# Loading, first norm, first modulation columns and input projection in one stage

## The chip, the cores and the metric

The kernel runs on one core of a Trainium2 chip. The core has TensorE (PE in the rows, with PEld for its weight loads), VectorE (DVE), ScalarE (ACT), GpSimd (POOL) and SyncE (SP, used here for issuing DMAs). The metric is the device time of one run in microseconds (us). The kernel before takes 2195.86 us, the median of three runs (2195.0 to 2195.89).

## The reference, cut to what matters

Two transformer blocks of two layers each are computed for 256 latent tokens and 256 context tokens of width 1024. The change touches only the first steps of the first layer. In the reference they are:

```
m_l = (silu(c) @ mod_w + mod_b)[:, None, :]        # 6 x 1024 values; shift and scale come first
m_c = silu(c_ctx) @ mod_w + mod_b
sh1_l, sc1_l, g1_l, sh2_l, sc2_l, g2_l = jnp.split(m_l, 6, axis=-1)
p_lat = _ada(x, norm1, sh1_l, sc1_l) @ w_in        # _ada = rmsnorm(x, g) * (1 + scale) + shift
p_ctx = _ada(ctx, norm1, sh1_c, sc1_c) @ w_in      # w_in is 1024 x 3328
```

## The kernel before

Activations lie transposed: a tile holds 128 of the 1024 features in its partitions and all 512 tokens in its free dimension, so XT, HT and OT have 8 tiles each (KT = 8) and PT has 32. Weights stream from memory through RING, which has four slots (SLOTS = 4); a slot holds 1024 x 256 weights, 1 MB. Matmuls of the projections are done in three passes for precision: a weight slot and the operand are each split into a rounded high part and a rest (high and low), and the passes are high by high, high by low and low by high (three_passes, L627 ff.). Of a slot there are two halves m, each with 8 k-tiles by 3 passes, 24 matmuls of 512 columns. The first input projection has 13 slots, so 26 halves and 624 matmuls.

The program is a row of stages. A stage (class Stage) is a block in which each engine has its own instruction list; at its end all engines meet, and no instruction of the next stage starts before. The first three stages are:

- load_stage (L358 ff.). SP issues the constants (1.4 MB), the tokens x and ctx (four tiles of 0.5 MB), the first four slots of the modulation weights (mod.fetch, L667), and WDG. ACT issues 31 small DMAs of vectors (rows of ROWS), c and c_ctx among them, then applies Silu to c and c_ctx. POOL issues 24 small DMAs. TensorE waits for the constants and for all 31 rows, transposes the three row tiles (L440), then waits for the tokens and transposes them (L447, 32 transposes). VectorE copies the results out of the PSUM banks (L457, L460), and derives small vectors, LAM among them.
- first_ada_stage (L713 ff.). ACT squares XT (L737), TensorE sums the squares with a matrix of ones (L752), ACT makes the root with Ln and Exp (L2611, L2617), DVE multiplies (L763). TensorE then adds up the modulation columns, one slot after another (Modulation.add, L678, 16 records a slot), each followed by a copy of the sums on ACT (copy, L686) and by small matmuls that turn them into columns (fold, L691). SP refills a ring slot when its sums are done: slots 4 to 7 of the modulation, then the first four slots of the projection's weights. At the end DVE forms MOD and AFF (L701, L708), and DVE (5 tiles, L771) and ACT (3 tiles, L746) scale and shift HT.
- project_stage (L781 ff.). ACT makes the high part of the first half slot (L560), then the high parts of the eight operand tiles (L564, OT_rounded); DVE makes the rests (L590 for the weights, L582 for the operand, HT_rounded). TensorE starts with the first tile of these (L632 to L634). The halves of weight slots alternate between two high buffers; ACT takes each finished bank to PT (L798). Some of the loop turns run in a hardware loop (turns).

After them comes diff_prepare_stage (L2411 ff.), and everything behind it is not touched. A class Part, used for the projections of later stages, does what project_stage does in straight-line code, with four high buffers (high4) and matmuls on L880 to L882.

Order is set by semaphores and by the order of the instructions on each engine; nothing reorders them at run time.

Of the kernel before, what the change touches and what calls it, by code (L numbers as in the profile page):

```python
# [34 lines left out]
P = 128  # L35
# [21 lines left out]
C_OVER = C_EPS + 4  # L57
# [10 lines left out]
C_FOLD = C_SINA + LAT  # L68
N_CONST = C_FOLD + 2

# [287 lines left out]
def load_stage(net, mod):  # L358

    nc, ins = net.nc, net.ins  # L360
    rows = net.SC[:, 0:3 * P].rearrange("p (g m) -> p g m", m=P)
    tokens = net.PT[:, 0:2 * NCH, :].rearrange("p t m -> p (t m)").rearrange("p (t d) -> p t d", d=D)
    with Stage(net, "load") as st:
        const_in, rows_in, x_in = st.sem("const_in"), st.sem("rows_in"), st.sem("x_in")
        small_in, zeroed = st.sem("small_in"), st.sem("wf_zeroed")
        turned, copied, cols_ready = st.sem("turned"), st.sem("copied"), st.sem("cols_ready")
        own = st.sem("dve_own")
        lam_exp, lam_sums, act_own = st.sem("lam_exp"), st.sem("lam_sums"), st.sem("act_own")
        smalls_in = net.smalls_in
        n_rows = sum(len(t) for t in ROWS)  # L370

        @st.sync
        def _(sp):
            sp.dma_start(net.CONST[:, :], ins["const_1"]).then_inc(const_in, 16)
            for t in range(2):
                sp.dma_start(tokens[:, t, :], ins["x"][0, P * t:P * t + P, :]).then_inc(x_in, 16)
            for t in range(2):
                sp.dma_start(tokens[:, 2 + t, :], ins["ctx"][0, P * t:P * t + P, :]).then_inc(x_in, 16)
            for n in range(SLOTS):
                mod.fetch(sp, n)  # L380
            w1 = ins["l1_w_in"]
            for at, col in ((0, 1536), (16, 3088)):
                sp.dma_start(net.WDG[:, :, at:at + 16],
                             w1[:, col:col + 16].rearrange("(t k) m -> k t m", k=P)).then_inc(small_in, 16)
            sp.wait_ge(small_in, 32)

        @st.scalar
        def _(act):
            n = 0
            for g, tile in enumerate(ROWS):  # L390
                r = 0
                for name, count in tile:
                    a = ins[name]
                    if len(a.shape) == 2:
                        a = a.rearrange("a b -> (a b)")
                    flat = a.rearrange("(t p) -> t p", p=P)
                    act.dma_start(rows[r:r + count, g, :], flat).then_inc(rows_in, 16)
                    r += count
            link = Chain(act, act_own)

            act.wait_ge(cols_ready, 3)
            act.wait_ge(zeroed, 2)
            for n, name in enumerate(("c", "c_ctx")):
                act.activation(mod.c[:, :, n], net.PAR[:, COL[name]:COL[name] + 8], ACT.Silu)

            act.wait_ge(lam_sums, 1)
            act.activation(net.LAM[:, 2:4], net.LAM[:, 0:2], ACT.Exp).then_inc(lam_exp, 1)

        @st.gpsimd
        def _(pool):  # L410
            pool.memset(net.WF[:, :, :, :], 0.0).then_inc(zeroed, 1)
# [4 lines left out]
            for n, name in enumerate(("l1_dt_bias_f", "l1_dt_bias_b", "l1_a_log_f", "l1_a_log_b",  # L416
                                      "l1_d_skip")):
                small.append((net.HEADROW[:, 8 * n:8 * n + 8], ins[name].partition_broadcast(P)))
# [87 lines left out]
def turns(engine, w, turn, straight=False, peel=False):  # L506
# [3 lines left out]
    for i in range(first):  # L510
        turn(i, range(SLOTS))
# [3423 lines left out]
```

## Time and profile before

| | before |
|---|---|
| median of 3 runs | 2195.86 us |
| profiled execution: own time / span | 2197.19 / 2195.40 us |
| busy share: TensorE, weight loads, VectorE, ScalarE, GpSimd | 89%, 77%, 55%, 38%, 14% |
| mean granted TensorE clock over the span | 0.938 of full |
| bytes read from memory | 251.28 MB, 115 GB/s over the span |

The span runs from the first to the last instruction, and all times in rows are counted from its start. The profile page cuts the span into 40 slices of 55 us. In the first, TensorE is busy 4 tenths and the DMA engines 7; in the second and third TensorE is busy 8 and 9 tenths, as the projection runs. The shares of the page are means over all stages, and so the rows below are taken from the first 72 us and from single stretches.

### The profile page before, as it was taken

The numbers are of one execution on the slowest core, as the hardware profiler recorded it, in microseconds if no ns is written. First come the engines' busy times: TensorE is split into PE (matmuls) and PEld (weight loads), VectorE is DVE, ScalarE is ACT, GpSimd is POOL, SyncE is SP. The second block draws the span as 40 slices with busy tenths as digits, with TensorE's granted clock in tenths as the row PEclk, the third lists the DMA queues.
The fourth block names the chain that finished last, engine by engine and source line by source line (L and its number), as shares of the span: only waits on it lengthen the run. The fifth ranks groups of instructions, "written<-read, shape, count | busy, mean of one in ns | idle before, by whom it ended". The sixth has DMA issues, their size and how long they took to land. (4 is left out here: it accounts for less than half of the span.)

```text
span 2195.4 us, 42104 instructions
## 1 busy us (share of the span) xinstructions
PE 1956.1 (89%) x18071; PEld 1693.2 (77%) x18071; DVE 1218.2 (55%) x2095; ACT 828.1 (38%) x1459; POOL 304.7 (14%) x350
## 2 busy tenths in 40 slices
PE   4899787888788999999999658999899999898997
PEld 2688454776766988888978548999868999768997
DVE  2321756546346752353565657874586765577753
ACT  2322356314223331222344124553365444364432
POOL 2000302421412100001200211101103001112001
PEclk9899796997999999999999858999999999999998
DMA  7421592003014322322233005555405556314543
GB/s 221 137 95 38 192 307 97 4 4 97 4 59 136 97 96 96 96 95 89 86 115 111 5 1 165 183 188 182 150 16 163 188 163 203 116 52 153 182 158 110
DMA packets 248857, 255.00 MB, mean 116 GB/s; under 512 B 6898, under 2 KB 247170, under 8 KB 248546
## 3 DMA queue, kind: packets, MB, share of 16 engines
q1 hardware_dynamic: 247200, 251.19, 35.7%
q8 instruction: 141, 2.31, 0.4%
q0 software_dynamic: 864, 0.98, 0.2%
q14 instruction: 42, 0.34, 0.1%
q10 hardware_dynamic: 610, 0.18, 0.0%
HBM read 251.28 MB, written 1.05 MB: 115 GB/s over the span
## 5 line engine op out<-in xcount | busy, mean ns | idle before, releaser
L860 DVE TENSOR_TENSOR RING_rounded<-RING,SC_rounded 128x1024 fp32r<-128x1024 f32 (+2 forms) x364 | 429.8, 1224 | 197.3 <-ACT SC_rounded L853 196.8
L880 PE MATMUL bank<-OT_rounded,SC_rounded 128*128 128x256 f32 (+1 forms) x1600 | 494.1, 309 | 21.8 <-DVE PT L1599 11.4
L881 PE MATMUL bank<-HT_rounded,SC_rounded 128*128 128x256 f32 (+1 forms) x1600 | 490.7, 307 | 0.0
L882 PE MATMUL bank<-OT_rounded,RING_rounded 128*128 128x256 f32 (+1 forms) x1600 | 489.0, 306 | 0.0
L853 ACT ACTIVATE SC_rounded<-RING 128x1024 fp32r<-128x1024 f32 (+2 forms) x364 | 346.5, 1003 | 325.6 <-DMA RING<-in_l_mlp_w 186.4
L880 PEld LDWEIGHTS bank<-OT_rounded,SC_rounded 128*128 128x128 f32 x1600 | 306.1, 191 | 41.6 <-issue 13.5
L882 PEld LDWEIGHTS bank<-OT_rounded,RING_rounded 128*128 128x128 f32 x1600 | 306.1, 191 | 15.4
L881 PEld LDWEIGHTS bank<-HT_rounded,SC_rounded 128*128 128x128 f32 x1600 | 306.2, 191 | 13.7
L880 PE MATMUL bank<-PT_rounded,SC_rounded 128*128 128x256 f32 (+1 forms) x896 | 277.8, 310 | 4.9 <-DVE RING_rounded L860 4.9
L881 PE MATMUL bank<-PT_rounded,SC_rounded 128*128 128x256 f32 (+1 forms) x896 | 276.8, 309 | 0.0
L882 PE MATMUL bank<-PT_rounded,RING_rounded 128*128 128x256 f32 (+1 forms) x896 | 276.1, 308 | 0.0
L880 PEld LDWEIGHTS bank<-PT_rounded,SC_rounded 128*128 128x128 f32 x896 | 168.6, 188 | 16.8 <-DVE RING_rounded L860 6.1
L882 PEld LDWEIGHTS bank<-PT_rounded,RING_rounded 128*128 128x128 f32 x896 | 168.5, 188 | 10.6
L881 PEld LDWEIGHTS bank<-PT_rounded,SC_rounded 128*128 128x128 f32 x896 | 168.5, 188 | 9.4
L881 PE MATMUL bank<-OT_rounded,SC_rounded 128*128 128x256 f32 (+1 forms) x336 | 101.8, 303 | 0.0
L880 PE MATMUL bank<-HT_rounded,SC_rounded 128*128 128x256 f32 (+1 forms) x272 | 84.6, 311 | 17.4 <-DVE OT_rounded L1787 8.7
L3172 DVE TENSOR_TENSOR SC<-SC,bank 128x512 f32<-128x512 f32 (+1 forms) x80 | 51.4, 684 | 75.4 <-PE bank L3063 75.0
L632 PE MATMUL bank<-OT_rounded,SC_rounded 128*128 128x512 f32 x208 | 83.9, 403 | 7.3 <-DVE HT_rounded L582 7.3
L590 DVE TENSOR_TENSOR RING_rounded<-RING,SC_rounded 128x1024 fp32r<-128x1024 f32 x26 | 31.8, 1226 | 101.5 <-ACT SC_rounded L560 101.5
L1126 DVE SCALAR_TENSOR_TENSOR XT<-bank,MOD,XT 128x256 f32<-128x256 f32 x48 | 21.4, 481 | 115.4 <-PE bank L882 115.4
L882 PE MATMUL bank<-HT_rounded,RING_rounded 128*128 128x256 f32 (+1 forms) x272 | 83.6, 307 | 0.0
L633 PE MATMUL bank<-HT_rounded,SC_rounded 128*128 128x512 f32 x208 | 83.5, 402 | 0.0
(527 smaller groups left out, 3224.9 us busy)
## 6 DMA issues: line engine op xcount, KB each, us to landing
RING<-in_l_mlp_w SPq DMA_DIRECT2D x64, 1024.0 KB, 5.2
RING<-in_l_mod_w SPq DMA_DIRECT2D x48, 1024.0 KB, 6.5
RING<-in_w_ffn_in SPq DMA_DIRECT2D x44, 1024.0 KB, 5.1
RING<-in_l_w_in SPq DMA_DIRECT2D x25, 1024.0 KB, 5.4
RING<-in_w_ffn_out SPq DMA_DIRECT2D x16, 768.0 KB, 4.4
RING<-in_w_in SPq DMA_DIRECT2D x10, 1024.0 KB, 5.3
RING<-in_w_ffn_out SPq DMA_DIRECT2D x16, 640.0 KB, 4.2
RING<-in_l_w_out SPq DMA_DIRECT2D x8, 1024.0 KB, 5.3
```

What stands on the lines that cost most here:

```text
L590: net.nc.vector.tensor_tensor(low, whole, net.high(s, m)[:, 0:w.kts[s], :].bitcast(F32), ALU.subtract).then_inc(sems.split_ready[m], 1)
L632: net.nc.tensor.matmul(bank[:, 0:n], high, x_high, start=start, stop=False)
L633: net.nc.tensor.matmul(bank[:, 0:n], high, x_low, start=False, stop=False)
L853: act.activation(net.high4(s, m)[:, 0:self.w.kts[s], :], net.ring_half(net.RING, s, m, self.w.kts[s]), ACT.Copy).then_inc(self.high_ready, 1)
L860: net.nc.vector.tensor_tensor(low, whole, net.high4(s, m)[:, 0:self.w.kts[s], :].bitcast(F32), ALU.subtract).then_inc(self.split_ready, 1)
L880: net.nc.tensor.matmul(bank[:, tokens], high, x_high, start=start, stop=False)
L881: net.nc.tensor.matmul(bank[:, tokens], high, x_low, start=False, stop=False)
L882: return net.nc.tensor.matmul(bank[:, tokens], low, x_high, start=False, stop=stop)
L1126: return nc.vector.scalar_tensor_tensor(into, bank[:, tokens], net.MOD[:, gate + tile, j:j + 1], into, ALU.mult, ALU.add)
L3172: nc.vector.tensor_tensor(inv, inv, bank, ALU.subtract).then_inc(doubled, 1)
```

## The change

The three stages become one, first_stage. In it:

- The constants are loaded in two pieces: the first 646 columns (330 KB, identity, ones, epsilons and the fold columns, which moved ahead for this) come first, the rest after the first four weight slots of the projection. WDG is loaded there too.
- c and c_ctx are waited for alone and turned first. 13 of the 31 row DMAs are issued by ACT before it waits for them, 18 after the Silu.
- The tokens are transposed into six banks (0 to 5). TensorE adds modulation slot 0 right behind them, then the squares of tiles 0 to 3, slot 1, the squares of tiles 4 to 7, slots 2 and 3, then transposes the three row tiles, then slots 4 to 7.
- ACT shifts the odd tiles of HT, DVE the even ones, tile by tile, each followed by its high part (ACT) and rest (DVE). The projection's first weight slot is split after tile 0, its second after tile 5.
- The first slot of the projection runs k-tile by k-tile with both halves side by side, each k-tile as its operand tile is ready. The other 12 slots run as halves. Part is used in place of project_stage, with four high buffers and six banks, in straight-line code.
- LAM's Exp moves behind the first slot of the projection.

The diff, cut (load_stage, first_ada_stage, project_stage and their helpers go; first_stage is new):

```diff
@@ constants @@
-C_OVER = C_EPS + 4
+C_FOLD = C_EPS + 4
+C_OVER = C_FOLD + 2
@@ first_stage @@
+        part = Part(net, st, "in0", w_in, Operand(OR, HR), banks=6)
+        @st.sync
+        def _(sp):
+            sp.dma_start(net.CONST[:, 0:C_OVER], ins["const_1"][:, 0:C_OVER]).then_inc(const_in, 16)
+            for n, name in enumerate(("x", "ctx")):
+                for t in range(2):
+                    sp.dma_start(tokens[:, 2 * n + t, :], ins[name][0, P * t:P * t + P, :]).then_inc(x_in, 16)
+            for n in range(n_first):
+                if n >= SLOTS:
+                    sp.wait_ge(mod.summed, n - SLOTS + 1)
+                mod.fetch(sp, n)
+            for s in range(SLOTS):
+                sp.wait_ge(mod.summed, n_first - SLOTS + s + 1)
+                net.fetch(sp, w_in, 0, s)
+            sp.dma_start(net.CONST[:, C_OVER:N_CONST], ins["const_1"][:, C_OVER:N_CONST]).then_inc(late_in, 16)
...
+            part.fetch_all(sp, None)
+            sp.wait_ge(late_in, 48)
...
+        @st.tensor
+        def _(pe):
+            pe.wait_ge(const_in, 16)
+            pe.wait_ge(c_in, 32)
+            nc.tensor.transpose(net.ps[6][:, 0:16], rows[0:16, 0, :], ident[0:16, 0:16]).then_inc(c_turned, 1)
+            pe.wait_ge(x_in, 64)
+            for f in range(KT):
+                if f >= 6:
+                    pe.wait_ge(copied, f - 5)
+                for t in range(4):
+                    last = nc.tensor.transpose(net.ps[f % 6][:, P * t:P * t + P],
+                                               tokens[:, t, P * f:P * f + P], ident)
+                last.then_inc(turned, 1)
+            pe.wait_ge(c_ready, 2)
+            mod.add(pe, 0, 0)
+            squares(range(4))
+            mod.add(pe, 1, 0)
+            squares(range(4, KT)).then_inc(summed, 1)
+            mod.add(pe, 2, 0)
+            mod.add(pe, 3, 0)
+            pe.wait_ge(rows_in, 16 * n_rows)
+            pe.wait_ge(copied, 6)
+            for g, tile in enumerate(ROWS):
...
+            for n in range(4, n_first):
+                mod.add(pe, n, 0)
+            mod.fold(pe, n_first - 1, 0)
+            for m in range(2):
+                part.ready(pe, 0, m)
+            for kt in range(KT):
+                pe.wait_ge(split_ready, kt + 1)
+                for m in range(2):
+                    step = part.passes(0, m, kt, everything)
...
+            for q in range(1, part.total):
+                for m in range(2):
+                    part.half(pe, q, m, everything)
+        @st.scalar
+        def _(act):
+            fetch_rows(places[:13])
+            act.wait_ge(c_turned, 1)
+            act.wait_ge(zeroed, 1)
+            for n in range(2):
+                act.activation(mod.c[:, :, n], net.ps[6][:, 8 * n:8 * n + 8], ACT.Silu).then_inc(c_ready, 1)
+            net.log_exp_loaded = False
+            fetch_rows(places[13:])
+            for t in range(KT):
+                act.wait_ge(copied, t + 1)
+                act.activation(square[:, t, :], net.XT[:, t, :], ACT.Square).then_inc(squared, 1)
+                if t == 3:
+                    mod.copy(act, 0)
+            load_log_exp(net, act)
+            mod.copy(act, 1)
+            mod.copy(act, 2)
+            act.wait_ge(summed, 1)
+            link(act.activation(rstd, total, ACT.Ln, scale=1.0 / D, bias=net.eps(EPS)))
+            act.activation(rstd, rstd, ACT.Exp, scale=-0.5).then_inc(rstd_ready, 1)
+            for n in range(3, n_first):
+                mod.copy(act, n)
+            act.wait_ge(aff_ready, 1)
+            for t in range(KT):
+                if t in by_act:
...
+                act.activation(OR[:, t, :], HT[:, t, :], ACT.Copy).then_inc(high_ready, 1)
+                if t in (0, 5):
+                    highs(t // 5)
+            for q in range(part.total):
+                highs(q + 2)
...
+        @st.vector
+        def _(dve):
...
+            link(mod.bias(dve, (0, n_first - 1), 0, n_first - 1))
+            mod.gain(0, 0).then_inc(aff_ready, 1)
+            dve.wait_ge(aff_ready, 1)
+            dve.wait_ge(normed, KT)
+            shift(0)
+            for t in range(KT):
+                if t % 2 == 0:
+                    shift(t + 2)
+                dve.wait_ge(high_ready, t + 1)
+                nc.vector.tensor_tensor(HR[:, t, :], HT[:, t, :], OR[:, t, :].bitcast(F32),
+                                        ALU.subtract).then_inc(split_ready, 1)
+                if t in (0, 5):
+                    lows(t // 5)
+            lows(2)
...
@@ program @@
-        load_stage(net, mod)
-        first_ada_stage(net, mod, w_in0)
-        project_stage(net, "in0", w_in0, Operand(OR, HR, HT), both, net.PT, None)
+        first_stage(net, mod, w_in0)
```

## Rows read from the trace of the kernel before

**Rows 1.** Waits of the first 80 us: who waited <- for whom: us, times, longest.
```profile
PE bank L440 <- DMA SC<-in_g_post_ffn: 22.0, 1, 22.0
```

**Rows 2.** Timeline of SP, first 190 us: start us, us of issuing, what, count.
```profile
1.21 0.89 SPq L376 DMA_DIRECT2D PT<-in_x  x2
2.14 1.14 SPq L378 DMA_DIRECT2D PT<-in_ctx  x2
3.33 19.22 SPq L667 DMA_DIRECT2D RING<-in_l_mod_w  x4
```

**Rows 3.** DMA issues at 1.8, 2.9, 3.4 and 44.7 us: size, us to landing.
```profile
PT<-in_x SPq DMA_DIRECT2D x1, 512.0 KB, 11.6
...
PT<-in_ctx SPq DMA_DIRECT2D x1, 512.0 KB, 14.4
...
RING<-in_l_mod_w SPq DMA_DIRECT2D x1, 1024.0 KB, 19.4
...
RING<-in_l_mod_w SPq DMA_DIRECT2D x1, 1024.0 KB, 5.1
```

**Rows 4.** Timeline of TensorE, 13 to 72 us: start, us, instruction, count, idle before.
```profile
22.57 5.30 PE L447 MATMUL bank<-CONST,PT 128*128 128x128 f32 x32
33.45 10.16 PE L752 MATMUL bank<-PT,CONST 128*128 128x512 f32 x16 [5.58 <-ACT PT L737]
43.54 1.07 PE L678 MATMUL bank<-RING,SC 128*32 128x256 f32 x16
45.32 0.61 PE L691 MATMUL bank<-CONST,SC 128*128 128x2 f32 x4 [0.71 <-ACT SC L686]
...
55.87 0.61 PE L691 MATMUL bank<-CONST,SC 128*128 128x2 f32 x4 [0.50 <-ACT SC L686]
...
59.64 1.01 PE L691 MATMUL bank<-CONST,SC 128*128 128x2 f32 x4 [0.50 <-ACT SC L686]
...
63.02 1.01 PE L691 MATMUL bank<-CONST,SC 128*128 128x2 f32 x4 [0.51 <-ACT SC L686]
71.37 0.76 PE L632 MATMUL bank<-OT_rounded,SC_rounded 128*128 128x512 f32 x1 [7.34 <-DVE HT_rounded L582]
```

**Rows 5.** Timeline of VectorE in the same stretch.
```profile
25.37 3.87 DVE L460 COPY XT<-bank 128x512 f32<-128x512 f32 x6 [0.16 <-PE bank L447]
...
69.40 1.23 DVE L590 TENSOR_TENSOR RING_rounded<-RING,SC_rounded 128x1024 fp32r<-128x1024 f32 x1 [1.57 <-ACT SC_rounded L560]
```

**Rows 6.** Timeline of ScalarE in the same stretch (ACTq: its DMA issues).
```profile
12.76 0.46 ACTq L397 DMA_DIRECT2D SC<-in_g_post_ffn  x1
...
43.65 0.69 ACT L2611 ACTIVATE SC<-bank,CONST 128x512 f32<-128x512 f32 x1 [5.32 <-PE bank L752]
...
64.51 3.06 ACT L746 ACTIVATE HT<-HT,MOD,AFF 128x256 f32<-128x256 f32 x6 [1.54 <-DVE AFF L708]
68.31 1.06 ACT L560 ACTIVATE SC_rounded<-RING 128x1024 fp32r<-128x1024 f32 x1 [0.74 <-PEq L193]
69.27 4.25 ACT L564 ACTIVATE OT_rounded<-HT 128x512 fp32r<-128x512 f32 x8
```

**Rows 7.** Stretches: length, busy us (count) by engine, granted clock, DMA share, GB/s.
```profile
34.00:37.00 3.00, 3.00 (x4) 1.01 (x3) 0.00 (x0) 3.00 (x6) 0.00 (x0) 0.50 0.00 0
40.00:43.50 3.50, 3.50 (x9) 1.33 (x7) 0.00 (x0) 0.00 (x0) 0.00 (x0) 1.00 0.00 0
50.00:56.00 6.00, 4.49 (x59) 2.48 (x59) 0.00 (x0) 1.15 (x3) 0.00 (x0) 1.00 1.10 350
60.00:64.00 4.00, 3.49 (x24) 2.08 (x23) 0.00 (x0) 0.38 (x1) 0.00 (x0) 0.50 1.10 348
75.00:77.00 2.00, 2.00 (x6) 1.57 (x5) 2.00 (x3) 0.42 (x1) 0.00 (x0) 0.50 0.00 0
80.00:100.00 20.00, 20.00 (x88) 16.09 (x87) 4.90 (x4) 6.04 (x8) 0.00 (x0) 1.00 0.26 81
920.00:940.00 20.00, 20.00 (x88) 16.08 (x87) 9.47 (x14) 4.69 (x7) 0.00 (x0) 1.00 0.22 73
```

More of the change, by code:

```diff
@@ L67 @@
 C_SINA = C_COSA + LAT
-C_FOLD = C_SINA + LAT
-N_CONST = C_FOLD + 2
+N_CONST = C_SINA + LAT
 C_DFTC = C_OVER
@@ L503, in feed @@
             net.fetch(sp, following, 0, s)
-def turns(engine, w, turn, straight=False, peel=False):
-    first = w.loops if straight else min(w.loops, 1) if peel else 0
-    for i in range(first):
-        turn(i, range(SLOTS))
-    if w.loops - first == 1:
-        turn(first, range(SLOTS))
-    elif w.loops > first:
-        with engine.Fori(first, w.loops) as i:
-            turn(i, range(SLOTS))
-    if w.tail:
-        turn(w.loops, range(w.tail))
 class Operand:
@@ L577, in low_on_dve @@
-def low_on_dve(net, dve, w, sems, x=None, take=None, straight=False, side=None):
-    def split(operand, before):
-        for t in range(operand.tiles()):
-            dve.wait_ge(sems.operand_high, before + t + 1)
-            net.nc.vector.tensor_tensor(operand.low[:, t], operand.whole[:, t], operand.high[:, t].bitcast(F32),
-                                        ALU.subtract).then_inc(sems.operand_split, 1)
-    def turn(i, slots):
-        for s in slots:
-            for m in range(2):
-                whole, low = (net.ring_half(ring, s, m, w.kts[s]) for ring in (net.RING, net.RINGR))
-                dve.wait_ge(sems.high_ready[m], SLOTS * i + s + 1)
-                net.nc.vector.tensor_tensor(low, whole, net.high(s, m)[:, 0:w.kts[s], :].bitcast(F32),
-                                            ALU.subtract).then_inc(sems.split_ready[m], 1)
-                if is_first(i, s) and m == 0 and x is not None and x.whole is not None:
-                    split(x, 0)
-                if side and isinstance(i, int) and i == 0 and s == 1 and m == 0:
-                    split(side, x.tiles())
-                if take and not is_first(i, s):
-                    take(*((i, s - 1) if s else (i - 1, SLOTS - 1)), m)
-    turns(dve, w, turn, straight, peel=True)
-    if take:
-        for m in range(2):
-            take(*w.last(), m)
```

369 lines of the change are left out of this document (131 added, 238 removed).

## The prediction

> **What bounds the kernel now.** I read the page's slices first: TensorE is the busy engine in all but a few of them, and the first slice is the poorest of the front end. Then I read the waits of the first 80 us, and then the timelines of SP, TensorE, DVE and ACT side by side. The program is a row of stages with a meeting at each end, so what lies behind the first projection keeps its own length, and a change of the front end is worth exactly the us by which the projection's end comes earlier. So I look for what each step of the front end waits for.
>
> TensorE does nothing until 21.96 us, when the last of the 31 row DMAs is there [rows 1]. The tokens had long landed: the second tile of x is issued at about 1.7 us and lands 11.6 us later, at 13.3; the last tile of ctx is issued at about 2.8 and lands 14.4 later, at 17.2 [rows 2, 3]. Then come 5.30 us of transposes to 27.9, 5.58 us of waiting for the meeting and the first square, and the squares' sums from 33.45 to 43.6, many of them at half clock (4 records stand in the 3 us from 34, 9 in the 3.5 us from 40, with one overlapping at each end) [rows 4, 7]. Eight slots of modulation follow from 43.54 to 64.03, one every 2.11 us ((55.87 - 45.32) / 5), the last two dearer [rows 4]. Then TensorE is idle for 7.34 us while HT is shifted, the stage ends, and the first weights and operand tiles are split; the projection starts at 71.37 [rows 4 to 6]. From there TensorE is never without work: 88 matmuls stand in 20 us, at clock 1.00 [rows 7]. The front end therefore is a chain (rows' DMA, transposes, squares, modulation, shift, split), not an engine's throughput, and shortening any link of it counts in full.
>
> **The change part by part.** I rebuild TensorE's order in the new stage from these durations.
>
> *Token landing.* Ahead of the last token in SP's order now stand 0.33 MB of constants and 2.1 MB of tokens, 2.43 MB. In the kernel before 2.46 MB (constants 1.41 MB, x 1.05 MB) were there when the second x tile landed, at 13.3 us, with the same small DMAs of ACT and POOL beside them [rows 2, 3]. So I take 13.3. The bounds are 17.2, the landing of before, and 11.5, if fewer of ACT's rows compete (18 of them are issued later). The rule that speaks against a gain from the order on SP's queue is in the Trainium skill, DMA: Bandwidth & Descriptors, section Queues, rings and completion order: each engine goes round its queues packet by packet, so being first on SP's queue doesn't hold POOL's and ACT's transfers back. The reading from before's own landing has that sharing in it already.
>
> *c and the Silu.* c and c_ctx are the first two of ACT's issues. The row DMA issued last, at 12.76, took 9.2 us to 21.96; a lone 1 MB slot took 5.1 [rows 1, 3, 6]. So c is there between 6.5 and 10.6 us; I take 8. ACT issues its 31 rows up to 13.2 us, 0.40 each from its first issue on, so its 18 late issues take 7.2 us, to 15.5 (18 at the late bound). The squares need copied tiles from 14.8 on and TensorE asks for them from 19.7 on; ACT makes one in 0.53 us. Both bounds are hidden. All rows are there by 15.5 + 9.2 = 24.7, and TensorE wants them at 32.
>
> *Transposes.* From 13.3, 5.3 us as before, to 18.6. All at half clock they would be 6.8: 32 times a quarter of the 0.85 that a record of four times the columns takes then, which is twice the 0.43 of the next paragraph. VectorE's copies take 0.65 a bank [rows 5] and follow at the same pace; six banks leave two waits, both for copies that are long done.
>
> *The rest of TensorE's chain to the last fold.* Modulation sums, 8 x 1.07 = 8.6. Folds, 8 x 0.57 = 4.6 (0.61 less the overlap with the next add; 1.07 + 0.54 + 0.50 is the period of 2.11). The squares' sums are 16 records; at full clock they stand 0.43 apart (8 spacings in 3.5 us), 6.9 us in all, where they took 10.2 [rows 4, 7]. The row transposes 0.7. Waits for ACT's copy of 0.50 at folds 2, 4, 5, 6 and 7, 2.5 us; at folds 0 and 1 the squares hide it, at fold 3 the row transposes. Sum 23.3, so the last fold ends at 18.6 + 23.3 = 41.9, against 64.03. The root costs TensorE nothing: the squares are summed by 28, Ln and Exp (0.7 each) sit between copies 2 and 3 on ACT, and DVE's eight products, a 512-column operation each like its copies, end by 37. A wait is added here: ACT's copy 0 stands ahead of squares 4 to 7 and waits for TensorE's first sum at 19.7; queued behind it are four squares, done at 22.3, and TensorE wants the first of them at 24.7.
>
> *The slots behind it.* A slot issued into an empty queue lands after 5.1 us, and slots follow each other at 350 GB/s, 3.0 us each [rows 3, 7]. Slot 0 has 3.48 MB ahead of and in it: it lands about 18 (between the 17.2 of 3.5 MB and the 22.7 of before [rows 2, 3]), slots 1 to 3 at about 21, 24 and 27. Slot 4 is issued when slot 0 is summed, 19.7, and lands at 30; slots 5, 6, 7 are issued at 24.7, 29.7, 31.9 and land at 33, 36, 39. TensorE wants them at 33, 35, 37 and 39.5. The projection's slot 0 is issued at 34.3 and lands at 42, and ACT wants it at 43.7. Covered, but slot 7 and the projection's slot 0 by only 1 to 2 us.
>
> *From the last fold to the first matmul.* Before: 7.3 us. Now: MOD and AFF 0.5 (64.03 to 64.51 [rows 4, 6]); DVE's shift of tile 0, 0.65; its high part on ACT, 0.53 (4.25 / 8); two weight highs, 2.1; the second rest, 1.23; 0.3 of handing over. Sum 5.3 [rows 5, 6]. TensorE must wait for both halves of the weights here where it waited for one, but neither for three shifted tiles nor for a meeting. After that a k-tile costs TensorE 6 matmuls, 2.6 us at half clock and 1.4 at full; ACT spends 1.55 on an odd tile (two shifts of 0.51 and 0.53) and 0.53 on an even one, plus 2.1 once for the second slot. ACT ends its eight tiles 10 us after tile 0, TensorE reaches the last 12 us after it starts: no wait.
>
> *The projection.* 624 matmuls as before. Part's straight code runs them at the same pace elsewhere: 88 in 20 us at 920, 88 at 80 [rows 7]. The first 5 to 6 us run at half clock in before and will again, as TensorE is idle for 5 us ahead of it. So its length stays. The later piece of the constants and WDG go behind four slots, 3 us of transfer at about 54; slot 4 is wanted only 45 us after the start. LAM's Exp, its table load and two stage meetings fall off the front; what is left of them lies under TensorE.
>
> *Sum.* Start of the projection 41.9 + 5.3 = 47.2, against 71.37: 24.2 us. In that sum no slot of modulation runs at half clock. In before the granted clock was 1.00 from 50 to 56 and 0.50 from 60 to 64 [rows 7]; the fall came some 13 us after TensorE had turned from dense squares to the sparse sums, and cost 1.3 us a slot (63.02 - 59.64 - 2.11). The sparse run now is 28.5 to 41.9, as long, so I charge one slot: 1.3. **Net 22.9 us.** Span 2195.4 - 22.9 = 2172.5, the profiled execution 2197.19 - 22.9 = 2174.3; against the median of the runs, 1.3 lower than the profiled one, 2173.0.
>
> **The rivals.**
>
> *The clock stays low in the front end.* The sums are sparse, and now they lie between the squares. For it: in before the clock fell in just such a stretch. The Trainium skill, TensorE: Matmul & The Clock Gate, section What's actually happening, says that the throttled state is the default and that activity releases it. Against it: the dense stretches (transposes, eight squares) lie only 1.1 and 1.6 us apart from 13.3 to 28.5, and in before the clock that was 0.50 from 34 to 37 was 1.00 from 40 on, within the dense squares [rows 7]. Price: transposes 6.8 for 5.3, squares 10.2 for 6.9 (their own row), and 1.3 for each of two to four slots more: 1.5 + 3.3 + 2.6 to 5.2, 7 to 10 us. Saving 13 to 16, time 2180 to 2183. Chance 0.13.
>
> *The DMA stream sets the start.* 11.9 MB have to land before the first weight slot can be split, and 1.2 MB of small ones; at 350 GB/s and 2 us of start that is 39.5, but the first 17 us of before moved less than that. If the stream is 4 us late, the projection starts at about 50 to 51. For: SP's issues of slots were held up in before (19.22 us for four [rows 2]). Against: in before slots landed at 350 GB/s whenever asked. Saving 19 to 21, 2175 to 2177. Chance 0.15.
>
> *The change gives nothing.* It would if the tokens or the rows were still what is waited for, and if the shift by tiles left the start where it was. The rows are wanted only at 32, so their old landing at 22 doesn't matter. Chance 0.01.
>
> *Slower.* The new start finds TensorE at half clock, and it stays there. The projection at half clock takes 0.43 for 0.23 us a matmul (75 to 77 against 80 to 100 [rows 7]), so each us of work at full clock becomes 1.8; the 22.9 us are gone when the clock stays low for some 50 us, two and a half slots. The place is the first slots, where waits for operand tiles could keep the engine sparse. In before the clock was 0.50 up to 77 and 1.00 from 80 on, and here too no wait is longer than a tile. Chance 0.02, time 2200 or more.
>
> **How the numbers follow.** Forecast (saving 20.5 to 26) 0.69, clock 0.13, DMA 0.15, nothing 0.01, slower 0.02. The range: below, tokens at 11.5 (1.8 us) and no slow slot (1.3), and a small shift elsewhere (1): 2169. Above, tokens at 17.2 (3.9 us) alone give 2177, and the clock's rival reaches 2183; cut so that 2 in 10 stay out, 2181. Two kernels can be told apart here from about 0.2%, 4.4 us: faster by more than that 0.96, within it 0.02, slower 0.02.
>
> **What would show it.** In the new profile: TensorE's first token transpose near 13.3 (17: the order on SP's queue gave nothing). The wait behind it on the first modulation slot under 1 us. Squares' records 0.43 apart. The last fold near 43, and before the projection one idle time of about 5 us put down to DVE's rests. ACT's first weight high not waiting for RING<-in_l_w_in (if it is, the DMA rival). The projection's end about 23 us earlier, and all stretches behind it of the old length. I would be wrong if transposes or squares show the half-clock spacing, if the first k-tiles have gaps on TensorE, or if a later stage has changed its length.

## The result, and the profile after

The changed kernel takes 2169.03 us, the median of four runs (2165.69 to 2171.72), against 2195.43 for the kernel before (four runs, 2192.89 to 2195.89): a ratio of 0.9881, 95% interval 0.9864 to 0.9898, 26 us faster. Six more executions of it on another occasion gave 0.9877 (0.9851 to 0.9904). The forecast was 2173.0, a saving of 22.9 us.

The profiled execution took 2167.82, its span was 2166.0. Its timeline of TensorE, to be held against [rows 4] (start, us, instruction, count, idle before):

```profile
5.19 0.26 PE L2147 MATMUL bank<-CONST,PT 16*128 16x16 f32 x1 [5.19 <-DMA PT<-in_c_ctx]
13.68 6.60 PE L2153 MATMUL bank<-CONST,PT 128*128 128x128 f32 x32 [8.23 <-DMA PT<-in_ctx]
20.21 1.07 PE L443 MATMUL bank<-RING,SC 128*32 128x256 f32 x16
21.21 3.70 PE L2142 MATMUL bank<-PT,CONST 128*128 128x512 f32 x8
...
26.18 3.70 PE L2142 MATMUL bank<-PT,CONST 128*128 128x512 f32 x8
...
41.18 1.07 PE L443 MATMUL bank<-RING,SC 128*32 128x256 f32 x16 [0.40 <-DMA RING<-in_l_mod_w]
42.75 0.61 PE L456 MATMUL bank<-CONST,SC 128*128 128x2 f32 x4 [0.50 <-ACT SC L451]
48.73 0.77 PE L549 MATMUL bank<-OT_rounded,SC_rounded 128*128 128x512 f32 x1 [5.37 <-DVE RING_rounded L529]
...
197.86 3.14 PE L2328 MATMUL bank<-PT,CONST 128*128 128x256 f32 x12 [1.00 <-PEq L193]
```

Here is to be seen: the tokens are turned from 13.68 on; there is no gap of 5.58 us behind the transposes any more; slot 7 of the modulation was waited for by 0.40 us; the last fold ends at 43.36 where it ended at 64.03; and the projection starts at 48.73, 22.6 us earlier. The last row is the first matmul of the next stage. In the kernel before it reads:

```profile
220.82 3.14 PE L2411 MATMUL bank<-PT,CONST 128*128 128x256 f32 x12 [0.99 <-PEq L193]
```

So 22.96 us were won when the changed code was done. The span is 29.4 shorter. The other 6.4 us come from behind it, where the code is the same; the first two experiments are about them.

Laid side by side with [rows 4], the 22.6 us at the projection's start are made up so: the tokens are turned 8.9 us earlier (at 13.68 for 22.57); the 5.6 us of waiting behind the transposes are gone; the squares' sums take 3.0 less (3.54 for each half, to the start of what follows, for 10.1 in one piece); the eight slots with their folds take 4.4 less (16.1 for 20.5, the row transposes now among them); and the wait ahead of the projection is 2.0 shorter (5.37 for 7.34). Against them stand transposes that took 1.2 more. Some 5.5 us of this are the clock and not the order as such: the 3.0 of the squares, which partly ran at half clock before, and 2.5 for the two slots that ran at half clock before and not here.

The stretches of the changed kernel around the projection's start (columns as in [rows 7]):

```profile
36.00:43.50 7.50, 5.45 (x64) 3.29 (x64) 2.98 (x12) 1.15 (x3) 0.00 (x0) 1.00 1.10 349
43.70:48.70 5.00, 0.00 (x0) 0.00 (x1) 4.53 (x8) 4.01 (x6) 0.00 (x0) 0.50 1.10 349
49.00:53.00 4.00, 4.00 (x10) 3.13 (x10) 3.74 (x8) 3.94 (x8) 0.00 (x0) 0.50 1.10 392
54.00:58.00 4.00, 4.00 (x19) 3.23 (x18) 3.66 (x4) 3.97 (x7) 0.00 (x0) 1.00 0.24 32
```

All eight slots ran at full clock; it fell when the last fold was over, and the projection's first 5 us ran at half. The DMA share is 1.1 up to 53 us: there the DMA engines always have work, and the 0.40 us for slot 7 are the first place where the stream of weights holds TensorE up.

### The profile page after: what moved, and what is told of

Same layout as the page of the kernel before. It is cut to its first block and busy times, and to the rows that moved or that the text cites. A ratio compares the mean times of both kernels' runs of the same rounds, so it can differ in the third digit from the quotient of the medians.

```text
span 2166.0 us, 41984 instructions
## 1 busy us (share of the span) xinstructions
PE 1941.1 (90%) x18072; PEld 1680.1 (78%) x18072; DVE 1215.8 (56%) x2093; ACT 828.2 (38%) x1460; POOL 294.6 (14%) x350
## 5 line engine op out<-in xcount | busy, mean ns | idle before, releaser
L529 DVE TENSOR_TENSOR RING_rounded<-RING,SC_rounded 128x1024 fp32r<-128x1024 f32 (+2 forms) x390 | 459.3, 1220 | 278.0 <-ACT SC_rounded L522 277.7
L549 PE MATMUL bank<-OT_rounded,SC_rounded 128*128 128x256 f32 (+1 forms) x1808 | 574.9, 318 | 27.2 <-DVE PT L1268 11.4
L550 PE MATMUL bank<-HT_rounded,SC_rounded 128*128 128x256 f32 (+1 forms) x1808 | 570.9, 316 | 0.0
L551 PE MATMUL bank<-OT_rounded,RING_rounded 128*128 128x256 f32 (+1 forms) x1808 | 569.0, 315 | 0.0
L522 ACT ACTIVATE SC_rounded<-RING 128x1024 fp32r<-128x1024 f32 (+2 forms) x390 | 372.4, 1006 | 322.5 <-DMA RING<-in_l_mlp_w 186.0
L549 PEld LDWEIGHTS bank<-OT_rounded,SC_rounded 128*128 128x128 f32 x1808 | 343.6, 190 | 56.2 <-issue 14.5
L551 PEld LDWEIGHTS bank<-OT_rounded,RING_rounded 128*128 128x128 f32 x1808 | 342.8, 190 | 25.5
L550 PEld LDWEIGHTS bank<-HT_rounded,SC_rounded 128*128 128x128 f32 x1808 | 343.4, 190 | 22.5
L550 PE MATMUL bank<-OT_rounded,SC_rounded 128*128 128x256 f32 (+1 forms) x336 | 101.1, 301 | 0.0
L549 PE MATMUL bank<-HT_rounded,SC_rounded 128*128 128x256 f32 (+1 forms) x272 | 84.1, 309 | 17.4 <-DVE OT_rounded L1456 8.8
L456 PEld LDWEIGHTS bank<-CONST,SC 128*128 128x128 f32 x192 | 31.5, 233 | 51.1 <-ACT SC L451 50.1
L549 PEld LDWEIGHTS bank<-HT_rounded,SC_rounded 128*128 128x128 f32 x272 | 52.5, 193 | 21.5 <-DVE RING_rounded L529 14.6
L550 PEld LDWEIGHTS bank<-OT_rounded,SC_rounded 128*128 128x128 f32 x336 | 64.5, 192 | 2.3
```

The lines of the kernel that those rows point to most:

```text
L456: last = self.nc.tensor.matmul(self.columns[:, 2 * (n - first) + m, :], self.rows[:, P * m:P * m + P], self.net.const(C_FOLD, 2), start=Tr ...
L522: act.activation(net.high4(s, m)[:, 0:self.w.kts[s], :], net.ring_half(net.RING, s, m, self.w.kts[s]), ACT.Copy).then_inc(self.high_ready, 1)
L529: net.nc.vector.tensor_tensor(low, whole, net.high4(s, m)[:, 0:self.w.kts[s], :].bitcast(F32), ALU.subtract).then_inc(self.split_ready, 1)
L549: net.nc.tensor.matmul(bank[:, tokens], high, x_high, start=start, stop=False)
L550: net.nc.tensor.matmul(bank[:, tokens], high, x_low, start=False, stop=False)
L551: return net.nc.tensor.matmul(bank[:, tokens], low, x_high, start=False, stop=stop)
```

## The experiments

Ends of stages are compared by two marks that every profile has: the projection's first matmul, and the first matmul of the stage behind it (called the mark). "Rest" is the span less the mark.

**The changed kernel again**, six executions.

> The changed kernel, nothing edited. In its first profile the projection started at 48.7 us and ended 23.0 us earlier than before, but the span was 29.4 us shorter and the median 26.4. My theory: the front end is worth 23.0 and the rest of the program, whose code is the same, varies by some 3 us from run to run with the granted clock; then the difference over five rounds is 21.5 to 24.5 us, and single times of one kernel spread over 4 us or more. Rival: the program behind the projection is shorter for good because it begins at another time; then the difference stays at 26 or more, and the stretch from the projection's end to the end is again 6 us shorter than in the kernel before.

The interval of the ratio, 0.9851 to 0.9904, is a difference of 21 to 33 us around 27; it holds both theories' numbers, and the six times of this one kernel lay between 2164.6 and 2176.9. Its profile:

```profile
37.44 0.69 PE L456 MATMUL bank<-CONST,SC 128*128 128x2 f32 x4 [0.51 <-ACT SC L451]
38.06 1.93 PE L443 MATMUL bank<-RING,SC 128*32 128x256 f32 x16
...
50.27 0.77 PE L549 MATMUL bank<-OT_rounded,SC_rounded 128*128 128x512 f32 x1 [5.38 <-DVE RING_rounded L529]
...
199.19 3.14 PE L2328 MATMUL bank<-PT,CONST 128*128 128x256 f32 x12 [1.00 <-PEq L193]
```

In this execution the last two modulation slots ran at half clock (1.93 for 1.07), and the mark came at 199.19. Against the first profile of the kernel before, the front end therefore is worth 21.6 to 23.0 us, depending on how many slots the clock falls on. The rest was 1968.6, as short as in the first profile (1968.1), so time alone couldn't decide.

**The kernel before again**, and the rest in all profiles.

> The kernel before, nothing edited, for a second profile. The stretch from the first matmul behind the projection to the end of the span was 1974.6 us in its first profile and 1968.1, 1968.6 and 1968.4 in the changed kernel's three (after, again, delay4), with 246, 230, 234 and 241 us of it at half clock. If this stretch only varies with the clock of the run, it comes out anywhere from 1966 to 1978 here, and its half-clock time goes with it. If the old front end makes it longer for good, it is 1973 or more again. The projection starts at 71.4, within 1.5.

The rest came out at 1972.7 and the projection started at 71.86. The mark came at 220.28, so that between the two profiles of each kernel 21.1 to 23.0 us lie. With the profiles of all runs the rest reads (us of it at half clock in brackets, summed from the records of the granted clock up to the end of the span; the expectation above has them about 2 us higher, as it counts a last record that reaches past that end):

| kernel | mark | rest | kernel | mark | rest |
|---|---|---|---|---|---|
| before | 220.82 | 1974.5 (244) | const_whole | 203.10 | 1975.6 (252) |
| before_again | 220.28 | 1972.7 (244) | rows_first | 205.71 | 1976.2 (246) |
| tokens_alone | 221.16 | 1971.5 (235) | sums_last | 199.85 | 1970.4 (248) |
| after | 197.86 | 1968.1 (228) | whole_operand | 202.26 | 1976.0 (246) |
| again | 199.19 | 1968.6 (232) | smalls_late | 194.87 | 1961.1 (219) |
| delay4 | 198.62 | 1968.4 (239) | best | 193.29 | 1975.1 (238) |
| busy_gap | 196.62 | 1972.9 (244) | busy_all | 195.57 | 1974.5 (246) |

With the old front end the mean of three is 1972.9, with the new one 1971.5 of eleven, and the eleven reach from 1961.1 to 1976.2. The rival, a rest that is 6 us shorter for good, falls. The same code behind the new front end has been longer than in any run of the old, and where the 6.4 us of the first pair arose can be read by following the same two VectorE instructions through the profiles: L1026 of the changed kernel (L1357 before), some 930 us behind the mark, and the L529 (L860) that comes 328 to 335 us after it. Between them, in the changed kernel's first profile, in its second, and in the kernel before (columns as in [rows 7]):

```profile
1129.46:1457.60 328.14, 279.75 (x2055) 258.27 (x2055) 222.12 (x405) 137.67 (x235) 40.53 (x42) 0.89 0.34 110
```
```profile
1124.02:1458.43 334.41, 286.79 (x2055) 264.48 (x2055) 222.00 (x405) 137.84 (x235) 39.44 (x42) 0.87 0.34 108
```
```profile
1149.82:1484.38 334.56, 287.04 (x2057) 264.73 (x2057) 222.40 (x404) 137.73 (x235) 40.29 (x42) 0.87 0.34 108
```

The first pair's difference is here, 6.4 us, with the same matmuls busy for 7 us longer (287.04 for 279.75), and the changed kernel's second execution doesn't have the shorter stretch. Of the fourteen profiles two, after and smalls_late, took 328.1 us for this stretch, with 75 us at half clock; the other twelve, of old and new front ends, took 334.2 to 335.0, with 85 to 92. Most of the other differences arise ahead of it: from the mark to its start it took 924 to 932 us, and from its end on 699 to 703. Over all profiles, rest and half-clock time go together (correlation 0.83), which fits the clock as the cause but doesn't show it.

So 21.1 to 23.0 us are shown to be the change. All times on record of the two kernels, 26 and 10, differ by 25.3 us in the mean (2195.1 and 2169.8), and an estimate of the 95% interval from their scatter is 22.4 to 28.2. What this has above the mark's difference is at the edge of the noise; a rest that is shorter by a few us is not excluded.

**A delay put in.**

> Four copies of one 512-column tile, 0.65 us each, stand on VectorE ahead of the first shift; they are extra work that only delays the projection. Both theories: the projection starts 2.6 us later, at 51.3, and ends 2.6 later. If the rest doesn't depend on when it begins, the time is 2.6 us above the changed kernel's of the same call, within its spread. If it does, the stretch behind the projection has another length than in the changed kernel, by 3 us or more and the same way in every run.

```profile
43.84 1.43 DVE L2286 COPY PT<-XT 128x512 f32<-128x512 f32 x4
```

The copies came one every 0.34 us, not 0.65: from SBUF to SBUF they are nearly twice as fast as the copies out of PSUM in [rows 5]. The projection started 1.4 later (50.09), but the mark came only 0.8 later (198.62), and the rest was 1968.4. The clock rose at 53.8 us here as in the changed kernel, so that 9 of the projection's matmuls stood 0.43 apart and not 12; that gave 0.6 of the 1.4 us back. So a delay ahead of the projection need not be paid in full, and a delay of 0.8 is too small to test the rest.

**The constants whole ahead of the tokens.**

```diff
-            sp.dma_start(net.CONST[:, 0:C_OVER], ins["const_1"][:, 0:C_OVER]).then_inc(const_in, 16)
+            sp.dma_start(net.CONST[:, :], ins["const_1"]).then_inc(const_in, 16)
...
-            sp.dma_start(net.CONST[:, C_OVER:N_CONST], ins["const_1"][:, C_OVER:N_CONST]).then_inc(late_in, 16)
```

> The changed kernel with the constants loaded whole (1.41 MB) ahead of the tokens, as before. My theory: the tokens land when 3.5 MB of SP's queue have, at 17.2 instead of 13.7, and the projection starts 3.5 us later, at 52.2 (within 0.7, and 1.3 more for each modulation slot at half clock). Rival: POOL's and ACT's transfers beside it decide when the tokens are there; then under 1 us.

```profile
18.07 5.46 PE L2152 MATMUL bank<-CONST,PT 128*128 128x128 f32 x32 [10.67 <-DMA PT<-in_ctx]
```

Tokens at 18.07, 4.4 us later, and the projection at 53.77, 5.0 later, with two slots touched by half clock and transposes that were 1.1 shorter. Against the changed kernel's second profile, which also had two such slots, it is 3.5. The theory stands. The price of 1.08 MB was 4.4 us and not 3.5, 246 GB/s; that POOL's and ACT's transfers take their share in just these us would explain it, and smalls_late below bears it out.

**All rows ahead of the tokens.**

```diff
             pe.wait_ge(x_in, 64)
+            pe.wait_ge(rows_in, 16 * n_rows)
...
-            fetch_rows(places[:13])
+            fetch_rows(places)
...
-            fetch_rows(places[13:])
```

> The changed kernel with all 31 row DMAs issued by ScalarE ahead of the Silu, and TensorE waiting for all of them before it turns the tokens, as before. My theory: the tokens are turned from 22 us on, 8.3 later, and the projection starts at 57 (within 1.5). Rival: the slots' landing or ScalarE's order was the bound, and the delay is partly taken up behind: under 6 us.

```profile
21.03 5.11 PE L2154 MATMUL bank<-CONST,PT 128*128 128x128 f32 x32 [16.38 <-DMA PT<-in_g_post_ffn]
...
56.67 0.77 PE L549 MATMUL bank<-OT_rounded,SC_rounded 128*128 128x512 f32 x1 [5.37 <-DVE RING_rounded L529]
```

7.4 us later at the tokens, 7.9 at the projection. Two modulation slots ran at half clock here; against the changed kernel's second profile, where two did as well, the projection is 6.4 later, so about 1 us of the delay is taken up (there TensorE waited 0.46 for slot 0, and the transposes took 5.50 for 5.11). This is the largest of the parts that were taken back one at a time.

**Squares first, sums behind them.**

```diff
             pe.wait_ge(c_ready, 2)
+            squares(range(KT)).then_inc(summed, 1)
             mod.add(pe, 0, 0)
-            squares(range(4))
             mod.add(pe, 1, 0)
-            squares(range(4, KT)).then_inc(summed, 1)
             mod.add(pe, 2, 0)
...
-                if t == 3:
-                    mod.copy(act, 0)
             load_log_exp(net, act)
-            mod.copy(act, 1)
-            mod.copy(act, 2)
...
-            for n in range(3, n_first):
+            for n in range(n_first):
                 mod.copy(act, n)
```

> The changed kernel with all eight squares' sums ahead of modulation slot 0, and ScalarE's copies 0 to 2 behind the root, as before. TensorE loses the squares as cover for the copies behind slots 0 and 1, 0.5 us each, and waits for Ln and Exp ahead of copy 0, 1.3; the sparse run of sums is 4 us longer, so one or two slots more may run at half clock, 1.3 each. I expect the projection's start 2 to 4.5 us later, at 51 to 53. Rival: the order of sums and squares is worth nothing, since TensorE has the same work: under 1 us.

The projection started at 51.49, 2.8 later. From the end of the transposes, which took 5.41 here for 6.60, to the last fold it is 3.9 longer. Of that, 1.2 are the waits for copies 0 and 1 (0.71 and 0.50; the 1.3 for Ln and Exp didn't appear). Slots 6 and 7 were waited for by 0.72 and 0.43 us, for 0.40 in the changed kernel: slots 4 and 5 are issued when slots 0 and 1 are summed, and that was 5.8 and 3.1 us later, so that the stream of weights ran dry for a while:

```profile
25.00:28.00 3.00, 2.29 (x21) 0.83 (x20) 0.44 (x1) 1.59 (x3) 0.00 (x0) 1.00 0.49 164
```

In the changed kernel these 3 us moved 348 GB/s. Slot 7 and the folds around it ran at half clock, 1.7 us. Adding slots early is worth the cover for two copies and the earlier refills, some 2 us, and what it does to the clock.

**The operand as a whole.**

```diff
-            for kt in range(KT):
-                pe.wait_ge(split_ready, kt + 1)
...
+            part.half(pe, 0, 0, everything, (split_ready, 1))
+            part.half(pe, 0, 1, everything)
...
+            act.wait_ge(shifted_by_act, 8)
+            act.wait_ge(shifted_by_dve, 4)
+            part.high(act, 0, 0)
+            for t in range(KT):
                 act.activation(OR[:, t, :], HT[:, t, :], ACT.Copy).then_inc(high_ready, 1)
-                if t in (0, 5):
-                    highs(t // 5)
+            part.high(act, 0, 1)
+            highs(1)
...
-            shift(0)
             for t in range(KT):
-                if t % 2 == 0:
-                    shift(t + 2)
+                shift(t)
+            part.low(dve, 0, 0)
...
```

> The changed kernel with the operand not taken by tiles: all eight tiles are shifted, then the first half of the weight slot is split, then the tiles, and the first slot runs as two halves. ScalarE shifts its four tiles in 4.3 us from 43.9, then 1.06 for the weights, VectorE 1.23 and 0.65: the wait ahead of the projection is 7.8 us instead of 5.4, and it starts and ends 2.4 later. Rival: the tile order only moves the waits into the first slot, and the projection ends within 0.7 us of where it did.

```profile
52.74 0.77 PE L549 MATMUL bank<-OT_rounded,SC_rounded 128*128 128x512 f32 x1 [7.61 <-DVE HT_rounded L2285]
```

The wait was 7.61 us instead of 5.37. Two modulation slots ran at half clock here, as in the changed kernel's second profile; against that one the mark came 3.1 later, 0.2 of it from ahead. The tile order is worth 2 to 3 us.

**The old kernel with the tokens turned first**, one part alone.

> The kernel before with one thing changed: TensorE turns the tokens first and the 31 rows behind them. If waiting for the rows was what cost, this alone moves the squares' sums by the 4.8 us between the tokens' landing and the rows', and the projection starts at 67. If the meeting at the end of the loading stage counts too, the rows' chain (transposes, copies, Silu, LAM) is now the last thing in that stage: rows turned at about 24, stage over at about 28 instead of 31.5, so only 3 us or less are won, and the projection starts at 68.5 to 70. The second is what I hold.

It won nothing: the projection started at 71.85, where the kernel before has 71.37 and 71.86. The timelines of TensorE, DVE and ACT, and SP's issues with their landing, tell why:

```profile
18.75 5.60 PE L440 MATMUL bank<-CONST,PT 128*128 128x128 f32 x32 [18.75 <-DMA PT<-in_ctx]
...
34.48 9.74 PE L750 MATMUL bank<-PT,CONST 128*128 128x512 f32 x16 [9.82 <-ACT PT L735]
```
```profile
28.20 0.15 DVE L477 TENSOR_SCALAR LAM<-LAM 128x1 f32<-128x1 f32 x1
```
```profile
27.11 2.86 SPq L383 DMA_DIRECT2D WDG<-in_l_w_in  x1
```
```profile
WDG<-in_l_w_in SPq DMA_DIRECT2D x1, 64.0 KB, 6.2
```
```profile
SPq L193 <- DMA WDG<-in_l_w_in: 3.3, 1, 3.3
```

VectorE ended its part of the loading stage at 28.35, the rows' chain was over, and yet the first square came at 33.8. What the stage waited for was the second WDG transfer, 64 KB for a much later stage: SP issued it at 27.11, behind four modulation slots, and it landed at 33.3. The last line is SP's wait for it, 3.3 us, ahead of the meeting. In the kernel before it is the same, with a wait of 3.4. The second WDG issue:

```profile
25.96 2.93 SPq L383 DMA_DIRECT2D WDG<-in_l_w_in  x1
```
```profile
WDG<-in_l_w_in SPq DMA_DIRECT2D x1, 64.0 KB, 6.3
```

It landed at 32.3, and ACT's first square started at 32.8. I had put that stretch down to the rows and LAM. They are not far off there: VectorE's last step for LAM ended at 31.0, 1.2 us ahead of WDG. With the tokens turned first it ended 2.7 earlier, and WDG landed 1.0 later. The rows' wait was real but hidden behind later ones. So the 8.9 us at the tokens and the 5.6 us behind the transposes are not two gains that could be had one by one: the new order pays because the stage's end, and with it the wait for WDG, went away too. That is read from the traces; a run of the old kernel with only WDG moved was not made.

**TensorE kept busy.**

```diff
+            pe.wait_ge(rstd_ready, 1)
             for n in range(4, n_first):
                 mod.add(pe, n, 0)
+                nc.tensor.matmul(net.ps[6][:, 0:256], net.const(C_ONES), net.CONST[:, 0:256], start=True, stop=True)
             mod.fold(pe, n_first - 1, 0)
+            for n in range(5):
+                nc.tensor.matmul(net.ps[6][:, :], net.const(C_ONES), net.CONST[:, 0:512], start=True, stop=True)
```

> TensorE gets matmuls on constants, into a bank nobody reads: one of 256 columns after each of the last four modulation slots, in its wait for ScalarE's copy, and five of 512 columns in the idle time between the last fold and the first matmul of the projection. If the clock falls at 43.7 us because the sums are sparse and the engine is then idle, it now stays at 1.00: the first 12 matmuls of the projection, which stood 0.43 apart, stand 0.23 apart, and the projection ends 2.3 us earlier, at 194.2; the time is 2 us below the changed kernel's. Rival: the clock falls all the same, and the extra matmuls only put off the projection's start, by up to 0.5 us: time the same or 0.5 us above.

TensorE's added wait for the root shows no idle time. The projection started 1.0 later (49.72), but at full clock:

```profile
34.35 1.92 PE L443 MATMUL bank<-RING,SC 128*32 128x256 f32 x16
36.20 1.22 PE L2171 MATMUL bank<-CONST 128*128 128x256 f32 x2
```
```profile
44.00:48.50 4.50, 4.50 (x14) 2.01 (x13) 3.68 (x9) 2.85 (x4) 0.00 (x0) 1.00 1.09 347
50.00:53.00 3.00, 3.00 (x14) 2.42 (x13) 2.77 (x7) 2.97 (x7) 0.00 (x0) 1.00 1.08 402
```

The 1.0 us come from a short fall of the clock at slot 4 (1.92 for 1.07), just ahead of the first of the extra matmuls, and after that it stayed at 1.00. Slot 0 had been waited for by 0.85 us, but its sum started at 20.12, as early as in the changed kernel. From its first matmul to the mark the projection took 146.9 us, where it took 149.1: 2.2 of the 2.3 us expected. The mark came 1.2 earlier than in the changed kernel. In the time (a median of 2171.4 in five executions, for 2169.5 of the changed kernel on the same occasion; a sixth took 4775 us, unexplained, and is left out) none of it can be seen.

> As busy_gap, and also: five matmuls of 512 columns on constants in the wait for the tokens (6 to 13.7 us), and the first k-tile's first three passes start when the first half of the weight slot is split, not both. If the clock is what makes the token transposes take 6.6 us, they run at the pace of VectorE's copies, 0.65 a bank, and their end moves from 20.2 to about 19; the projection's first matmul moves ahead by 1.2 more, and it ends at 192 to 192.5, 4 to 4.5 us earlier than in the changed kernel. Rival: the transposes keep their pace, the extra matmuls delay them: no gain there, projection's end at 193 to 194.

The transposes took 3.72 us instead of 6.60, but TensorE then waited 2.52 for modulation slot 0. That landed at 20.5; in the other profiles of this order that waited for it, with POOL's transfers where they were, it landed between 19.6 and 20.7. The projection started at 47.56, 1.2 earlier, and the mark came at 195.57, 2.3 earlier; 4 had been expected. The clock was the transposes' bound and the DMA stream the next one.

**POOL's small DMAs held back**, and the version with all of it.

```diff
+            pool.wait_ge(mod.summed, 5)
             for into, of in small:
                 pool.dma_start(into, of).then_inc(smalls_in, 16)
```

> The changed kernel with POOL's 24 small DMAs (1 MB) held back until modulation slot 4 is summed. My theory: they share the DMA engines with the tokens, and 1 MB of the 3.6 MB that arrive by 13.7 us is theirs: the tokens land at 11.2 (within 0.7), TensorE no longer waits 0.4 us for slot 7, and the projection starts 2 to 3.5 us earlier, at 45.3 to 46.8. Rival: SP's queue is served at its own pace, and the tokens land at 13.7 as before.

```profile
10.53 6.12 PE L2154 MATMUL bank<-CONST,PT 128*128 128x128 f32 x32 [5.57 <-DMA PT<-in_ctx]
...
46.70 0.76 PE L549 MATMUL bank<-OT_rounded,SC_rounded 128*128 128x512 f32 x1 [7.44 <-DVE RING_rounded L529]
```
```profile
ACT SC_rounded L522 <- DMA RING<-in_l_w_in: 2.0, 1, 2.0
```

The tokens landed 3.15 us earlier. The last fold was 4.1 earlier, but 2.0 were lost where the held-back transfers met the projection's first slot. The projection started 2.0 earlier, and the mark came at 194.87, 3.0 earlier, as the clock rose after fewer of the projection's matmuls. The time of this one execution, 2157.85, owes more to its rest, the shortest of all, than to the edit. By the Trainium skill, DMA: Bandwidth & Descriptors, section Queues, rings and completion order, engines go round their queues packet by packet, and this run agrees: POOL's 1 MB on another queue cost SP's queue 3.15 us.

> smalls_late and busy_all together (three matmuls on constants in the last gap, four in the wait for the tokens), and the first weight slot's high parts ahead of the shift on ScalarE, its first rest right behind the shift of tile 0 on VectorE, the second behind that tile's rest. Tokens at 11.2, last fold at 39 to 40, the projection's first matmul at 43 and at full clock; its end, and the first matmul behind it, at 190 (188.5 to 191.5) against 197.9. The time is some 8 us below the changed kernel's, 31 below the kernel before. Rival: the DMA stream is the bound now; then the first weight slot is waited for on ScalarE and the gain is 4 us or less.

The mark came at 193.29, 4.6 us earlier than in the changed kernel and 27.5 than in the one before, and not at 190: TensorE waited 2.1 us for modulation slot 7 and ACT 2.1 for the first weight slot, both while POOL's transfers ran, and slot 7 then ran at half clock. The median of its five times was 2169.45, ratio 0.9886 (0.986 to 0.9912) to the kernel before, with a rest of 1975.1 in its profile. That it beats the changed kernel is seen at the mark and not in the times: busy_gap, busy_all and best have their marks 1.2, 2.3 and 4.6 us earlier, and medians of 2171.4, 2170.2 and 2169.5, for 2169.0 and 2169.5 of the changed kernel. That a mark so much earlier is paid out in the time is argued, not shown. Holding POOL's transfers back until the first weight slots are there was not tried.

## Why the prediction was right

The mechanism was right: the front end is a chain, and what was forecast for its links can be found in the new profile. That the net agreed to 0.1 us is partly luck: two terms missed by more than a us each, and the misses cancelled.

- *Tokens at 13.3.* 13.68. The reading from the bytes ahead in SP's queue held to 0.4 us. The small transfers' share is in the reading and was large, as smalls_late shows.
- *c and the Silu hidden.* c was there at 5.19, below my lower bound of 6.5; nothing hung on it.
- *Transposes 5.3.* 6.60 and 5.50 in the changed kernel's two profiles, and 5.1 to 6.7 in the seven others without extra matmuls ahead of them. In the first profile this term was 1.2 us too small. The bound of 6.8 was the right upper end: how much runs at half clock differs between executions.
- *Slot 0 at 18.* It landed at 19.6 in the second profile and was waited for by 0.46 us. The term was 1.6 us or more too small, and cost little only since the transposes were slow as well; in busy_all, where they were not, it cost 2.52.
- *TensorE's chain of 23.3.* From 20.21 to 43.36 it took 23.15, the 0.40 for slot 7 included. The squares' records stand 0.43 apart as they should.
- *Last fold to first matmul 5.3.* 5.37, ended by the weights' second rest, as worked out.
- *One slot at half clock.* None in the first profile, two in the second; the fall's place is not fixed. In the first profile the 1.3 us charged for it and not needed paid for the transposes' 1.2: that is luck.
- *The projection's length unchanged.* From first matmul to mark 149.1 and 148.9 in the new, 149.45 and 148.4 in the old.
- *Net 22.9.* 22.96 at the mark. The step with no term in the sum was the rest, which I let be constant but for 1 us: it varies by 15 us between profiles, and the measured saving of 26 has 3 us of that in it. The range's lower end of 2169 was met by the median of 2169.03, and that too is luck: two of its four times lie below. With what the profiles show now it should have been some 4 us lower.
- *Why the loading stage ended when it did* was not asked. The prediction has the 5.58 us down as waiting for the meeting and the first square, and what the meeting waited for last was WDG. The sum didn't suffer, as it was built on what TensorE waits for in the new order, and WDG had left it.
- The DMA rival was right in its mechanism: the stream ran at 349 GB/s from 20 us on and made TensorE wait 0.40. It decided wherever other links were shortened (2.52 us in busy_all, 2.0 in smalls_late, 2.1 twice in best).

## What to carry to other kernels

A stage that waits for its transfers ends with the last of them, also one that only a much later stage wants: look for the DMA that lands just ahead of the next stage's first instruction before crediting a wait inside the stage. A new order of the same work can be forecast to a us or two in each term by rebuilding one engine's list from measured durations, if each of its waits is given a landing or a copy with its own time. When the sum then agrees much better than the terms, look for errors that cancel. A difference that arises in code that wasn't touched is followed up by a second profile of the same kernel, stretch by stretch. Small transfers on another queue delayed the first large ones here, by 3.15 us for 1 MB; where a step is bound by its first data, hold them back, but not into the next moment that a transfer is waited for.

## What the runs showed of the hardware

- The code behind the change, the same in all kernels, took 1961.1 to 1976.2 us in fourteen profiles, with 219 to 252 us at half clock. Single times of one kernel spread over 12 us. One stretch of it, with the same 2055 matmuls, took 328.1 us with 75 us at half clock, or 334.4 with 85, in two executions of one kernel.
- TensorE's first transposes are spaced as at half clock though the granted clock is given as 1.00 from 0 us. After 7 us of matmuls on constants the 32 transposes took 3.72 us (busy_all), after 6 us 3.66 (best), instead of 5.1 to 6.7. The Trainium skill, TensorE: Matmul & The Clock Gate, section What's actually happening, has the throttled state as the default; this agrees, and the value 1.00 ahead of the first record can't be read as granted.
- The clock fell within the modulation sums, at 37.8 us in the changed kernel's second profile, though TensorE had no idle time above 0.51 us since 19.6.
- 128x512 copies on VectorE came one every 0.34 us from SBUF to SBUF (delay4) and one every 0.6 from PSUM (busy_all).
